# Squares of the first block's last norm on ScalarE at the second mixer's entry, and one weight split moved inside the layer norm

## The chip, the core and the metric

The kernel is one program on one core of a Trainium2 chip. Its engines run their own instruction streams in order and meet only at semaphores: TensorE (PE in the profile, PEld its weight loads) multiplies matrices into PSUM banks, VectorE (DVE) and GpSimd (POOL) do elementwise arithmetic, ScalarE (ACT) evaluates functions, and SyncE (SP) issues the loads from memory. The metric is the device time of one execution in microseconds. Times inside the kernel count from the start of the profiled span.

## What is computed

Two transformer blocks, one behind the other, on 256 tokens of width 1024. The first block (feed forward, a mixer, feed forward) ends in an RMS norm, and the second block begins with one of its own on that output, with a scale and a shift made from `c`:

```python
def first_block(x, ...):
    ...
    h = h + 0.5 * swiglu_ffn(rmsnorm(h, ffn2_norm[layer]), ffn2_w_in[layer], ffn2_w_out[layer])
    return rmsnorm(h, final_norm)

def token_mixer(h, ...):
    z = h @ w_in
    u_glu, q_lat, kv_lat, k_r, gate_logits = jnp.split(z, IN_SPLIT, axis=-1)
    ua, ub = jnp.split(u_glu, 2, axis=-1)
    u = ua * jax.nn.sigmoid(ub)
    u = causal_depthwise_conv_2(u, conv_w, conv_b)
    u = jax.nn.silu(layer_norm(u, conv_norm_g, conv_norm_b))
    y_a = u @ w_conv_out
    ...
    y_b = o @ w_attn_out
    return (g_a * y_a + g_b * y_b) @ w_out

def second_block(x, ...):
    h = rms_norm(x, g_pre_mix[l]) * (1.0 + scale1) + shift1
    y = token_mixer(h, ...)
    x = x + gate1 * rms_norm(y, g_post_mix[l])
    ...
```

## The kernel before

Activations lie transposed: 8 tiles of 128 channels by 256 tokens. Every weight passes in slabs of 128 x 2048 values through three slots (`SLOTS = 3`). For each slab SyncE loads `raw`; ScalarE rounds it to `wh` (`cast`); VectorE makes the remainder `wl = raw - wh` (`sub`, here called the weight split); TensorE multiplies the three products high x high, high x low, low x high (`wide`, 48 products a slab). Inputs are held as such pairs too: `xh` from ScalarE, `xl` from VectorE. A load waits until the slot's last split is done, so a split is also what frees `raw` for the slab three further on.

Nothing schedules the work but the order in which each engine's code is written; every wait is a semaphore count (`wait_ge(*at(name, n))`).

**The entry of the second mixer.** The first block's residual `resid` comes out of the second feed forward in four pairs of tiles (`ffn2_resid`). Two column sums of it are needed. The g sums (`g_stat`), of squares times the final gain, give the second block's norm of the first block's normed output directly: ScalarE makes eight squares (`fg_sq`, line 997), VectorE adds three pairs, TensorE sums them with a matrix of ones into bank 6 (line 2321), ScalarE takes the root, VectorE the reciprocal (`inverse("g")`), then per tile VectorE, ScalarE and VectorE make `h`, `xh`, `xl` (lines 1630, 1003, 1636), and the first gated slab takes the tiles as they come (`by_tile`). Eleven filler products (`keep_busy(11, 4)`, lines 2045 to 2050) stand between the sums and that slab. The f sums (`f_stat`), of the plain squares, are needed much later for the first block's own output: GpSimd makes four pairs of squares (`squares`, lines 658 and 736) behind the rotation angles, TensorE sums them into bank 1 behind the second gated slab (line 2041), and ScalarE copies them to `std` (`f_kept`, line 1027) in the gated unit's second step.

**The gated unit and the long convolution.** Eight slabs give four gated pairs of tiles (`glu`): ScalarE's sigmoid, VectorE's product. The 31 taps are shared out: VectorE does tiles 2 to 5 (lines 1647 to 1656), GpSimd tiles 0, 1, 6 and 7 (lines 738 to 762) behind `glu` 1, with 18 of its taps scaled by ScalarE (`scale_taps`, line 1015), which may be at most three ahead of GpSimd's addition (`tap_added`). VectorE adds the last six taps of tiles 6 and 7 once GpSimd is through (line 1764, behind `long_conv`), which gives `conv_done`.

**The layer norm.** TensorE works through the four `attn_out` slabs; behind the second one it sums the convolution's columns (`ln_mean`, line 2473, behind `conv_done`), behind the third their squares (`ln_stat`, line 2479). VectorE takes the mean off (`centre`), splits three slabs (s+3, s+4 and s+5: the last `attn_out` slab and the first two of `conv_out`), makes the reciprocal of the root and scales; then ScalarE (silu and `xh`, lines 1179 and 1182) and VectorE (`xl`, line 1793) go tile by tile, and TensorE's first `conv_out` slab takes the tiles as they come.

The order in VectorE's code there is:

```python
            centre()
            sub(s + 3)
            sub(s + 4)
            sub(s + 5)
            inverse("ln", rstd[:, :], kr_raw)
```

## Time and profile before

| | us |
|---|---|
| median of 3 runs | 1033.26 |
| lowest, highest | 1033.26, 1034.24 |
| the profiled execution, its own time | 1032.48 |
| span of that execution, first to last instruction | 1030.7 |
| TensorE busy | 1015.1 (98%) |
| VectorE busy | 794.2 (77%) |
| ScalarE busy | 497.3 (48%) |
| GpSimd busy | 510.5 (50%) |

The profile's rows are of one execution, whose time is 0.78 us below the median. A timeline row gives the start and the length in us, the engine, the line, the operation and its tiles, how many instructions are merged, and in brackets how long the engine was idle before and who released it. Tiles go by the names of the memory they lie in: many buffers share `work`, and `ps` is any PSUM bank. A product of two full-precision operands (the column sums, the fillers) appears as two passes, so five sums read as x10 there and eleven fillers as x22. Lengths of TensorE's records overlap; the distance of two starts is what one costs.

### The profile page before, as it was taken

How to read it: one execution, taken by the hardware profiler on the slowest of the kernel's cores; microseconds unless marked ns; L12 is line 12 of the kernel's file. 1: busy time of each engine (PE TensorE's matmuls, PEld its weight loads, DVE VectorE, ACT ScalarE, POOL GpSimd, SP SyncE). 2: the span in 40 equal slices, each digit the busy share in tenths (PEclk: the TensorE clock that was granted, in tenths of full speed). 3: DMA queues.
4: the chain of work that ended last, by engine and by line, in shares of the span. 5: the costliest groups of instructions: out<-in, count | busy, mean ns of one | idle time of the engine just before them, and what ended most of it. 6: DMA issues, size and time to landing. Idle time of an engine off the chain costs nothing.

```text
span 1030.7 us, 19098 instructions
## 1 busy us (share of the span) xinstructions
PE 1015.1 (98%) x7801; PEld 971.7 (94%) x7801; DVE 794.2 (77%) x799; ACT 497.3 (48%) x578; POOL 510.5 (50%) x300
## 2 busy tenths in 40 slices
PE   9999999999999999999999999999999999999997
PEld 7999999998999899999999999998999978899886
DVE  5777777699886678878677859998898787667764
ACT  6443433477532463443343656667576454343432
POOL 4576757510043027557577999999930004314400
PEclk9999999999999999999999999999999999999999
DMA  9968677646340256677677365672236517675641
GB/s 273 320 207 269 216 255 234 213 138 182 93 154 1 93 194 212 219 258 230 230 243 243 92 195 149 155 227 94 83 116 197 178 60 229 229 235 184 218 149 41
DMA packets 165997, 188.33 MB, mean 183 GB/s; under 512 B 10574, under 2 KB 155548, under 8 KB 165820
## 3 DMA queue, kind: packets, MB, share of 16 engines
q1 hardware_dynamic: 165580, 186.13, 56.8%
q0 software_dynamic: 192, 1.36, 0.4%
q8 instruction: 35, 0.57, 0.2%
q10 hardware_dynamic: 176, 0.14, 0.1%
q14 instruction: 14, 0.11, 0.0%
HBM read 186.58 MB, written 1.05 MB: 182 GB/s over the span
## 4 chain that ended last, share of the span: by engine, by line
PE 93%; DVE 4%; ACT 1%; issue 1%; DMA 0%; ACTq 0%; DVEq 0%
PE ps L1966 56%; PE ps L2010 11%; PE ps L2018 9%; PE ps L2243 2%; PE ps L1977 2%; PE ps L2189 2%; PE ps L2365 1%; PE ps L2114 1%; DVE wl L1270 1%; PE ps L2409 1%; PE ps L2058 1%; PE ps L2407 1%; PE ps L2379 1%; PE ps L2396 1%; PE ps L2048 0%
## 5 line engine op out<-in xcount | busy, mean ns | idle before, releaser
L1966 PE MATMUL ps<-xh,wh 128*128 128x256 f32 x1208 | 345.3, 286 | 3.4 <-DVE xl L1793 1.9
L1966 PE MATMUL ps<-xl,wh 128*128 128x256 f32 x1208 | 341.7, 283 | 0.0
L1966 PE MATMUL ps<-xh,wl 128*128 128x256 f32 x1208 | 341.6, 283 | 0.0
L1275 DVE TENSOR_TENSOR wl<-raw,wh 128x2048 fp32r<-128x2048 f32 x78 | 251.5, 3224 | 63.3 <-ACT wh L789 63.3
L1966 PEld LDWEIGHTS ps<-xh,wh 128*128 128x128 f32 x1208 | 231.5, 192 | 7.1 <-issue 3.9
L1966 PEld LDWEIGHTS ps<-xl,wh 128*128 128x128 f32 x1208 | 231.6, 192 | 0.5
L1966 PEld LDWEIGHTS ps<-xh,wl 128*128 128x128 f32 x1208 | 231.6, 192 | 0.0
L789 ACT ACTIVATE wh<-raw 128x2048 fp32r<-128x2048 f32 x78 | 148.9, 1911 | 148.2 <-PE ps L1966 148.2
L1270 DVE TENSOR_TENSOR wl<-raw,wh 128x2048 fp32r<-128x2048 f32 (+1 forms) x74 | 181.9, 2464 | 39.1 <-ACT wh L783 38.6
L647 POOL TENSOR_TENSOR ada_raw<-ada_raw,c_act 128x2048 f32<-128x2048 f32 x24 | 87.6, 3648 | 217.3 <-DMA ada_raw<-in_w_ada 212.2
L783 ACT ACTIVATE wh<-raw 128x2048 fp32r<-128x2048 f32 (+1 forms) x74 | 138.9, 1882 | 70.3 <-PE ps L1966 56.2
L1966 PE MATMUL ps<-yh,wh 128*128 128x256 f32 x480 | 137.6, 287 | 0.0
L1966 PE MATMUL ps<-yl,wh 128*128 128x256 f32 x480 | 135.8, 283 | 0.0
L1966 PE MATMUL ps<-yh,wl 128*128 128x256 f32 x480 | 135.8, 283 | 0.0
L650 POOL TENSOR_TENSOR ada_raw<-ada_raw 128x1024 f32<-128x1024 f32 x24 | 99.5, 4145 | 1.9
L1966 PEld LDWEIGHTS ps<-yh,wh 128*128 128x128 f32 x480 | 92.1, 192 | 0.6 <-issue 0.4
L1966 PEld LDWEIGHTS ps<-yl,wh 128*128 128x128 f32 x480 | 92.1, 192 | 0.1
L1966 PEld LDWEIGHTS ps<-yh,wl 128*128 128x128 f32 x480 | 92.1, 192 | 0.0
L2010 PE MATMUL ps<-fh,wl 128*128 128x256 f32 x320 | 89.6, 280 | 0.0
L2010 PE MATMUL ps<-fh,wh 128*128 128x256 f32 x320 | 89.6, 280 | 0.0
L2010 PE MATMUL ps<-fl,wh 128*128 128x256 f32 x320 | 89.5, 280 | 0.0
L680 POOL TENSOR_TENSOR work<-work 128x256 f32<-128x256 f32 x13 | 12.6, 971 | 132.7 <-ACT work L806 69.5
(407 smaller groups left out, 1840.0 us busy)
## 6 DMA issues: line engine op xcount, KB each, us to landing
raw<-in_ffn_w_in SPq DMA_DIRECT2D x43, 1024.0 KB, 7.5
ada_raw<-in_w_ada SPq DMA_DIRECT2D x24, 1024.0 KB, 5.3
raw<-in_ffn_w_out SPq DMA_DIRECT2D x22, 1024.0 KB, 5.0
raw<-in_w_in SPq DMA_DIRECT2D x18, 1024.0 KB, 5.4
raw<-in_w_mlp_in SPq DMA_DIRECT2D x16, 1024.0 KB, 5.5
raw<-in_w_mlp_out SPq DMA_DIRECT2D x16, 1024.0 KB, 4.9
raw<-in_w_mix_in SPq DMA_DIRECT2D x14, 1024.0 KB, 5.4
raw<-in_w_mix_out SPq DMA_DIRECT2D x4, 1024.0 KB, 5.3
```

The source lines that it names most:

```text
L647: pool.tensor_tensor(ada_raw[:, :, :], ada_raw[:, :, :], c_act[:, :].unsqueeze(2).to_broadcast([P, KT, 256]), ALU.mult).then_inc(S("ada_pa ...
L650: pool.tensor_tensor(flat[:, 0:1024], flat[:, 0:1024], flat[:, 1024:2048], ALU.add).then_inc(S("ada_part"), 1)
L783: act.activation(wh[:, s % SLOTS, 0:n], raw[:, s % SLOTS, 0:n], ACT.Copy).then_inc(high_done, 1)
L789: act.activation(wh[:, s % SLOTS, :], raw[:, s % SLOTS, :], ACT.Copy).then_inc(high_done, 1)
L1270: dve.tensor_tensor(wl[:, s % SLOTS, 0:n], raw[:, s % SLOTS, 0:n], wh[:, s % SLOTS, 0:n].bitcast(F32), ALU.subtract).then_inc(low_done, 1)
L1275: dve.tensor_tensor(wl[:, s % SLOTS, :], raw[:, s % SLOTS, :], wh[:, s % SLOTS, :].bitcast(F32), ALU.subtract).then_inc(low_done, 1)
L1966: mm = pe.matmul(bank[:, m * T:(m + 1) * T], w[:, k, m * P:(m + 1) * P], r[:, k, :], start=(m == 0 and k == 0 and j == 0), stop=(k == KT - ...
L1977: mm = pe.matmul(bank[:, m * T:(m + 1) * T], w[:, k, m * P:(m + 1) * P], r[:, k, :], start=(m == 0 and k == 0 and j == 0), stop=(k == KT - ...
L2010: mm = pe.matmul(ps[m // 2][:, (m % 2) * T:(m % 2 + 1) * T], w[:, k, m * P:(m + 1) * P], r[:, k, :], start=False, stop=False, skip_group_c ...
L2018: mm = pe.matmul(ps[n][:, :], r[:, k, tk * P:(tk + 1) * P], w[:, k, half * 512:(half + 1) * 512], start=False, stop=stop, skip_group_check ...
L2189: mm = pe.matmul(unit(bank, u % 4), lhs(u), rhs(u), start=(u % 4 == 0), stop=True, skip_group_check=True)
L2243: mm = pe.matmul(bank[:, u % 4 * CH // 2:(u % 4 + 1) * CH // 2].rearrange("p (a s) -> p a s", s=2 << i), unit(lhs, u), half_columns(unit(r ...
```

## The change

The four GpSimd squares are taken out. ScalarE makes the same four pairs of plain squares, each behind the two gained squares of its pair. TensorE sums them into bank 7, two products behind each of the first three g sums and two behind the last one; the eight sums behind the second gated slab go, and the fillers are two in place of eleven. ScalarE's copy of the sums stands behind the tiles of `xh` at the entry, and TensorE's second slab of the gated unit's second step waits for it before it writes bank 7. In the layer norm, the split of slab s+5 moves from ahead of the reciprocal to behind the second tile's low part.

```diff
--- before.py
+++ after.py
@@ -733,7 +733,6 @@
                     ins.then_inc(S("angles"), 1)
                 else:
                     step(ins)
-            squares("f", "ffn2_resid", f_squares)
             pool.wait_ge(*at("ada_taken", ADA_EARLY))
             for g, group in enumerate(POOL_TILES):
                 pool.wait_ge(*at("glu", group[-1] // 2 + 1))
@@ -995,12 +994,17 @@
             for t in range(KT):
                 act.wait_ge(*at("ffn2_resid", t // 2 + 1))
                 act.activation(qn[:, t, :], resid[:, t, :], ACT.Square, scale=final_coef[:, t:t + 1]).then_inc(S("fg_sq"), 1)
+                if t % 2:
+                    act.activation(f_squares[:, t - 1:t + 1, :], resid[:, t - 1:t + 1, :], ACT.Square).then_inc(S("f_sq"), 1)
 
             act.wait_ge(*at("g_stat", 1))
             act.activation(std[:, :], ps[6][:, 0:T], ACT.Sqrt, scale=1.0 / D, bias=eps_sq).then_inc(S("g_std"), 1)
             for t in range(KT):
                 act.wait_ge(*at("h_f", t + 1))
                 act.activation(xh[:, t, :], scaled_input(t), ACT.Identity, bias=ada[:, t:t + 1]).then_inc(S("h_xh"), 1)
+            act.wait_ge(*at("g_rstd", 1))
+            act.wait_ge(*at("f_stat", 1))
+            act.activation(std[:, :], ps[7][:, 0:T], ACT.Copy).then_inc(S("f_kept"), 1)
             cast(FIRST["glu"] + 2)
             taps_ahead = list(range(len(ACT_TAPS)))
 
@@ -1020,11 +1024,6 @@
                 scale_taps((0, 1, 1, 1)[n])
                 cast(s + 3)
                 scale_taps((0, 1, 1, 1)[n])
-                if n == 1:
-
-                    act.wait_ge(*at("g_rstd", 1))
-                    act.wait_ge(*at("f_stat", 1))
-                    act.activation(std[:, :], ps[1][:, 0:T], ACT.Copy).then_inc(S("f_kept"), 1)
                 act.wait_ge(taken, s + 2)
                 if n:
                     act.wait_ge(*at("glu", n))
@@ -1781,7 +1780,6 @@
             centre()
             sub(s + 3)
             sub(s + 4)
-            sub(s + 5)
             inverse("ln", rstd[:, :], kr_raw)
             dve.wait_ge(*at("ln_cen", 4))
             for b in range(4):
@@ -1791,6 +1789,8 @@
             for t in range(KT):
                 dve.wait_ge(*at("c_xh", t + 1))
                 dve.tensor_tensor(xl[:, t, :], conv[:, t, :], xh[:, t, :].bitcast(F32), ALU.subtract).then_inc(S("c_xl"), 1)
+                if t == 1:
+                    sub(s + 5)
                 if t == 5:
                     mix_b(3)
             sub(s + 6)
@@ -2316,19 +2316,30 @@
             ffn("ffn2", "n3", yh, yl, ("mix_resid", 4))
 
 
+            def first_block_sums(b):
+
+                pe.wait_ge(*at("f_sq", b + 1))
+                for k in (2 * b, 2 * b + 1):
+                    mm = pe.matmul(ps[7][:, 0:T], ones, f_squares[:, k, :], start=(k == 0), stop=(k == KT - 1), skip_group_check=True)
+                if b == 3:
+                    mm.then_inc(S("f_stat"), 1)
+
             for k in (0, 2, 4, 6, 7):
                 pe.wait_ge(*(at("g_add", k // 2 + 1) if k < 6 else at("fg_sq", k + 1)))
                 mm = pe.matmul(ps[6][:, 0:T], ones, qn[:, k, :], start=(k == 0), stop=(k == KT - 1), skip_group_check=True)
+                if k < 6:
+                    first_block_sums(k // 2)
             mm.then_inc(S("g_stat"), 1)
-            keep_busy(11, 4)
+            first_block_sums(3)
+            keep_busy(2, 4)
             for n in range(4):
                 s = FIRST["glu"] + 2 * n
                 if n >= 2:
                     pe.wait_ge(*at("glu", n - 1))
                 wide(s, ps[4 + 2 * (n % 2)], xh, xl, "h_xl" if n == 0 else None, one, by_tile=(n == 0))
+                if n == 1:
+                    pe.wait_ge(*at("f_kept", 1))
                 wide(s + 1, ps[5 + 2 * (n % 2)], xh, xl)
-                if n == 0:
-                    column_sums("f", lambda k: f_squares[:, k, :], KT, ps[1][:, 0:T], ("f_sq", 1), by_pair=True)
             s = FIRST["lat"]
             pe.wait_ge(*at("glu", 3))
             for n in range(3):
```

In these rows `work` is the memory of the squares and of the convolution, `con` the table with the matrix of ones, `att_col` the gains. TensorE's stream at the entry, before: the g sums and the fillers, and, where rows are left out, the first two gated slabs and then the f sums.

```order
L2114 MATMUL ps<-xh,wl 128x256
L2321 MATMUL ps<-work,con 128x256 x5
L2048 MATMUL ps<-con 128x256 x11
L1966 MATMUL ps<-xh,wh 128x256
...
L1966 MATMUL ps<-xh,wl 128x256
L2041 MATMUL ps<-work,con 128x256 x8
L1966 MATMUL ps<-xh,wh 128x256
```

The same place after, where an x counts products:

```order
L2114 MATMUL ps<-xh,wl 128x256
L2329 MATMUL ps<-work,con 128x256
L2323 MATMUL ps<-work,con 128x256 x2
L2329 MATMUL ps<-work,con 128x256
L2323 MATMUL ps<-work,con 128x256 x2
L2329 MATMUL ps<-work,con 128x256
L2323 MATMUL ps<-work,con 128x256 x2
L2329 MATMUL ps<-work,con 128x256 x2
L2323 MATMUL ps<-work,con 128x256 x2
L2048 MATMUL ps<-con 128x256 x2
L1966 MATMUL ps<-xh,wh 128x256
```

Six f sums now stand ahead of the last g sums, two behind them, and nine fillers and the later eight sums are gone. ScalarE's stream at the entry, before:

```order
L846 ACTIVATE att_col<-att_col,con 128x8
L997 ACTIVATE work<-resid,att_col 128x256 x8
L1000 ACTIVATE std<-ps,con 128x256
L1003 ACTIVATE xh<-ps,ada 128x256 x8
L783 ACTIVATE wh<-raw 128x2048 x2
...
L1015 ACTIVATE ada_raw<-work,vec 128x256 x2
L1027 ACTIVATE std<-ps 128x256
L1031 ACTIVATE hid<-ps 128x512
```

and after:

```order
L845 ACTIVATE att_col<-att_col,con 128x8
L996 ACTIVATE work<-resid,att_col 128x256 x2
L998 ACTIVATE work<-resid 128x512
L996 ACTIVATE work<-resid,att_col 128x256 x2
L998 ACTIVATE work<-resid 128x512
L996 ACTIVATE work<-resid,att_col 128x256 x2
L998 ACTIVATE work<-resid 128x512
L996 ACTIVATE work<-resid,att_col 128x256 x2
L998 ACTIVATE work<-resid 128x512
L1001 ACTIVATE std<-ps,con 128x256
L1004 ACTIVATE xh<-ps,ada 128x256 x8
L1007 ACTIVATE std<-ps 128x256
```

Four squares of 512 stand among the eight of 256, and the copy to `std` comes right behind the tiles of `xh`. VectorE's stream in the layer norm, before:

```order
L1738 TENSOR_TENSOR work<-work,rstd 128x512 x4
L1270 TENSOR_TENSOR wl<-raw,wh 128x2048 x3
L1292 RECIPROCAL rstd<-work 128x256
L1788 TENSOR_TENSOR work<-work,rstd 128x512 x4
L1775 TENSOR_TENSOR work<-ps,con 128x512
L1793 TENSOR_TENSOR xl<-work,xh 128x256 x6
L1775 TENSOR_TENSOR work<-ps,con 128x512
L1793 TENSOR_TENSOR xl<-work,xh 128x256 x2
L1270 TENSOR_TENSOR wl<-raw,wh 128x2048
```

and after:

```order
L1737 TENSOR_TENSOR work<-work,rstd 128x512 x4
L1269 TENSOR_TENSOR wl<-raw,wh 128x2048 x2
L1291 RECIPROCAL rstd<-work 128x256
L1786 TENSOR_TENSOR work<-work,rstd 128x512 x4
L1774 TENSOR_TENSOR work<-ps,con 128x512
L1791 TENSOR_TENSOR xl<-work,xh 128x256 x2
L1269 TENSOR_TENSOR wl<-raw,wh 128x2048
L1791 TENSOR_TENSOR xl<-work,xh 128x256 x4
L1774 TENSOR_TENSOR work<-ps,con 128x512
L1791 TENSOR_TENSOR xl<-work,xh 128x256 x2
L1269 TENSOR_TENSOR wl<-raw,wh 128x2048
```

The third weight split went from ahead of the reciprocal to between the second and the third low part.

## Rows read from the trace of the kernel before

**Rows 1.** page, section 4: shares of the chain that ended last, by engine

```profile
PE 93%; DVE 4%; ACT 1%; issue 1%; DMA 0%; ACTq 0%; DVEq 0%
```

**Rows 2.** timeline of TensorE, entry: start us, us, engine, line, op, out<-in, xcount

```profile
573.55 1.02 PE L2321 MATMUL ps<-work,con 128*128 128x256 f32 x4
...
576.23 4.91 PE L2048 MATMUL ps<-con 128*128 128x256 f32 x22
580.78 0.47 PE L1966 MATMUL ps<-xh,wh 128*128 128x256 f32 x1
```

**Rows 3.** chain in order of time, entry: start us, us, what, xcount

```profile
592.64 3.45 PE ps L2041 x16
```

**Rows 4.** timeline of GpSimd, squares and long convolution

```profile
585.95 8.13 POOL L661 TENSOR_TENSOR work<-resid 128x512 f32<-128x512 f32 x4
...
596.01 2.55 POOL L750 TENSOR_TENSOR work<-work,ada_raw 128x512 f32<-128x512 f32 x1 [0.74 <-ACT ada_raw L1015]
...
602.45 0.94 POOL L754 TENSOR_SCALAR con<-work,vec 128x256 f32<-128x256 f32 x2
...
604.86 2.85 POOL L754 TENSOR_SCALAR con<-work,vec 128x256 f32<-128x256 f32 x2
...
750.18 3.33 POOL L757 TENSOR_TENSOR work<-work,con 128x512 f32<-128x512 f32 x1
```

**Rows 5.** timeline of VectorE, last taps of the long convolution

```profile
753.55 5.46 DVE L1764 SCALAR_TENSOR_TENSOR work<-work,vec 128x256 f32<-128x256 f32 x12 [1.20 <-POOL work L757]
```

**Rows 6.** chain in order of time, ahead of the mean sums

```profile
741.95 17.26 PE ps L1966 x144
```

**Rows 7.** timeline of ScalarE, entry

```profile
571.16 1.71 ACT L997 ACTIVATE work<-resid,att_col 128x256 f32<-128x256 f32 x4
...
576.42 0.47 ACT L1000 ACTIVATE std<-ps,con 128x256 f32<-128x256 f32 x1 [1.04 <-PE ps L2321]
```

**Rows 8.** timeline of VectorE, entry

```profile
577.09 1.75 DVE L1292 RECIPROCAL ps<-std 128x256 f32<-128x256 f32 x1
...
585.25 0.48 DVE L1636 SCALAR_TENSOR_TENSOR xl<-ps,ada,xh 128x256 fp32r<-128x256 f32 x1 [0.15 <-ACT xh L1003]
```

**Rows 9.** timeline of ScalarE, latents of the second mixer

```profile
646.41 0.91 ACT L1015 ACTIVATE ada_raw<-work,vec 128x256 f32<-128x256 f32 x2 [1.75 <-POOL work L750]
...
650.51 1.28 ACT L1052 ACTIVATE work<-work 128x1280 f32<-128x1280 f32 x1
```

**Rows 10.** timeline of TensorE, sums of the latents

```profile
653.52 1.46 PE L2343 MATMUL ps<-work,con 128*128 128x256 f32 x6
```

**Rows 11.** timeline of VectorE, layer norm

```profile
766.25 7.23 DVE L1270 TENSOR_TENSOR wl<-raw,wh 128x2048 fp32r<-128x2048 f32 x3
773.40 1.74 DVE L1292 RECIPROCAL rstd<-work 128x256 f32<-128x256 f32 x1
...
778.19 1.10 DVE L1793 TENSOR_TENSOR xl<-work,xh 128x256 fp32r<-128x256 f32 x3
```

**Rows 12.** timeline of ScalarE, layer norm

```profile
771.17 0.47 ACT L811 ACTIVATE work<-ps,con 128x256 f32<-128x256 f32 x1 [0.61 <-PE ps L2479]
...
775.90 0.60 ACT L1179 ACTIVATE work<-work,vec 128x256 f32<-128x256 f32 x1 [2.56 <-DVE work L1788]
...
782.51 0.59 ACT L1179 ACTIVATE work<-work,vec 128x256 f32<-128x256 f32 x1
```

**Rows 13.** timeline of TensorE, first slab of conv_out

```profile
778.75 0.36 PE L1966 MATMUL ps<-xh,wh 128*128 128x256 f32 x1 [1.87 <-DVE xl L1793]
...
784.06 0.39 PE L1966 MATMUL ps<-xh,wh 128*128 128x256 f32 x1
```

**Rows 14.** timeline of the SP queue, loads behind the layer norm

```profile
773.50 22.22 SPq L492 DMA_DIRECT2D raw<-in_w_out  x4
```

**Rows 15.** timeline of TensorE, its last product

```profile
1024.46 0.39 PE L2018 MATMUL ps<-wl,xh 128*128 128x512 f32 x1
```

**Rows 16.** stretches: us, busy of five engines, PEclk, DMA share, GB/s

```profile
1026.00:1028.00 2.00, 0.00 (x0) 0.00 (x0) 1.96 (x5) 0.20 (x1) 0.00 (x0) 0.77 0.42 159
```

## Prediction

> **What bounds the kernel now.** I read the views in this order: the chain that ended last, TensorE's waits, then the timelines of each engine around the two places that the change touches. The chain is TensorE for 93% [rows 1], and at the second mixer's entry it is TensorE without a break: the squares' column sums, eleven filler products, two gated-unit slabs, then the eight sums of the first block's squares [rows 2, 3]. So products taken off TensorE are worth their length, as long as nothing else becomes late. The second thing to see is that GpSimd has a fixed stream of its own: its share of the long convolution starts once the first gated pair exists, runs from 596.01 to 753.51 and waits for nobody [rows 4]. VectorE stands idle 1.20 us for its end, adds the last taps until 759.01 [rows 5], and TensorE finishes the three slabs ahead of the layer norm's mean sums at 759.21 [rows 6]. Two independent streams meet there within 0.2 us. Whatever moves TensorE earlier than GpSimd's stream is lost there.
>
> **Entry, TensorE.** Five sums, eleven fillers and eight later sums (24 products) become 5 + 8 + 2 = 15. A product is two passes, 3.45 / 16 = 0.216 us each [rows 3]. The eight sums behind the second slab go: -3.45 us. But six of them now stand ahead of the last product of the g sums. Before, the sums start at 573.55 and the next product starts at 576.23 [rows 2]. Now 11 products have to pass: 573.55 + 22 x 0.216 = 578.30, which is 2.07 later. ScalarE isn't what holds them: its 256-wide squares follow each other by 0.41 [rows 7], four added 512-wide ones cost some 0.6 each (a 512-wide ScalarE square or copy is bounded by two 256-wide ones, 0.86), and its last square ends near 576.9, before TensorE gets there.
>
> From there the chain is serial: ScalarE's root ended at 576.89 [rows 7], the reciprocal started at 577.09, held 0.20 by a weight split [rows 8]; that slack is used up, so the reciprocal moves by 2.07 - 0.20 = 1.9, and all of h with it. Before, the first product started at 580.78 on low parts that were ready [rows 2] and the last low part ended at 585.73 [rows 8]; TensorE spends 17.26 / 144 = 0.12 a product [rows 6], 0.72 a tile, so it reached the last tile at about 586.0. Now that part ends at 587.6 and TensorE starts its last tile 0.14 later, 587.77: the first slab, and the second with it, end **1.75 us later**. The fillers are gone as cover: four products remain behind the g sums (578.30 + 4 x 0.43 = 580.0), and TensorE is idle from there to 582.4.
>
> So TensorE goes on after the second slab at +1.75 - 3.45 = **-1.70**, but the first gated pair, which needs the second slab, is at **+1.75**.
>
> **Entry, GpSimd.** The four squares leave it (8.13 us from 585.95, [rows 4]), but its next work needs the gated pair and a tap scaled by ScalarE: it already waited 0.74 us for that tap [rows 4]. The freed time buys nothing; the stream moves by +1.75. At 157.5 us of length it ends at 755.3 and VectorE's last taps at 760.8. ScalarE's copy of the sums moves to an idle place ahead of a cast (about 0.3 us, followed by a wait for TensorE): nothing.
>
> **Between.** ScalarE may scale a tap only three ahead of GpSimd, and at 646.41 it already waited 1.75 us for it [rows 9]. It now waits until 648.2; queued behind are a cast, the last latent copies and their square, which ended at 651.79 [rows 9] and would now end near 652.75. TensorE's latent sums stood at 653.52 [rows 10] and want to start at 651.8: about 1.0 us is lost, TensorE runs at -0.7 from there. The same mechanism can't make it later than GpSimd's own +1.75.
>
> **The mean sums.** TensorE arrives at 759.1 - 0.7 = 758.4 and waits until 760.9. It starts the mean sums at +1.75 to +1.85, I take **+1.8**. The -3.45 is gone and the serial delay of the entry stays.
>
> **The weight split in the layer norm.** VectorE did three splits in 7.23 us, then the reciprocal at 773.40 [rows 11], whose root was ready at 771.64 [rows 12]. With two ahead, it starts at about 771.7: -1.7. The first low part came 4.79 us after the reciprocal started [rows 11], so 776.5; the second follows by 0.34. Then the moved split (7.23 / 3 = 2.4 us) stands before the third: third low part at about 779.6 to 780.0. TensorE (which starts at 777.0 in place of 778.75, after a 1.87 us wait [rows 13]) does two tiles, stands 1.5 us, and starts its last tile at 780.1 + 5 x 0.72 = 783.7. Before, that start was 784.06 [rows 13], paced by ScalarE's tile pairs at (782.51 - 775.90) / 7 = 0.94 [rows 12]. Gain **0.4 us**: the wait is cut in two rather than removed. Bounds: -1.7 if the moved split were hidden, 0 if it cost all. I take the row-by-row value. The first of the four loads issued from 773.50 [rows 14] is freed by the moved split and goes some 6 us later; its rounding waits for a slab that ends 96 products after 778.75, so about 6 us of slack remain.
>
> **Sum.** +1.8 - 0.4 = +1.4 us. On the profiled execution: span 1030.7 + 1.4 = 1032.1, time 1032.48 + 1.4 = 1033.9; on the median 1033.26 + 1.4 = **1034.6**. 0.2% is 2.07 us, about what a measurement can tell from no change.
>
> **Rivals.**
> (A) *The saved products carry through* (faster). If GpSimd's stream shortened by 3.4 us, -1.7 - 0.4 = -2.1 would remain: 1031.1. It could only shorten by fewer collisions with VectorE: a pair of its taps takes 0.94 alone and 2.85 beside a weight split [rows 4], so two fewer. The number of splits inside the stream is the same; little speaks for it.
> (B) *One collision more* (slower): +1.9 on the stream that sets the mean sums, 1036.5. The alignment of the two engines shifts by 1.75 + 1.70 = 3.45 us, so collisions fall anew; it decides from +0.7 us.
> The Trainium skill (SBUF — State Buffer, Who interferes with whom) says that a VectorE instruction with two SBUF inputs and a GpSimd one that reads SBUF exclude each other and that issue order decides who blocks; it has no ruling on the sum, and this trace agrees by the 2.85 beside 0.94.
> (C) *TensorE's clock falls* (slower). Two new idle stretches of some 2.4 us stand at 580 and at 758.5. In this trace the granted clock is 1.00 (2.4 GHz) through a wait of 1.87 us [rows 13], but at the end, the last product over at 1024.85 [rows 15], it averages 0.77 over 1026 to 1028 [rows 16], so it had fallen to its half (1.2 GHz) by about 1027.1, 2.2 us after work stopped. At half clock each pass takes twice 0.216. Work at half clock behind either gap is on the path: between 0 and the 3.45 us of sixteen passes, I take the middle, 1.7: 1036.3, and 1038.0 if both gaps are hit.
> The Trainium skill (TensorE: Matmul & The Clock Gate, What's actually happening) says that an idle stretch sends the clock back to 1.2 GHz and that where it falls varies from run to run. By that rule, C comes in some executions and not in others.
> (D) *The change does nothing measurable at both places* (the sums hidden, the split neutral): 1033.3.
>
> **Chances.** Forecast 0.46 (own range 1033.2 to 1035.3). A 0.08. B 0.15. C 0.27. D 0.04. Faster by over 0.2% (below 1031.2): A, 0.08. Within 0.2%: forecast and D, 0.50. Slower (above 1035.3): B and C, 0.42. The range leaves out A and the case of both gaps: 1032.0 to 1037.4.
>
> **What would show it.** In the profile after: the root of the g sums starts 2.07 us after 576.42; TensorE's first slab starts near 582.4 after an idle stretch; GpSimd's first tap addition near 597.8; TensorE waits some 2.4 us ahead of the mean sums, released by VectorE's last taps (line 1763); the reciprocal 1.7 us nearer the root, and two waits of some 0.4 and 1.5 us in the first conv_out slab. The forecast is wrong if GpSimd's stream isn't some 157.5 us long, or starts before the gated pair, if the wait at the mean sums is missing, or if the granted clock drops below 1.00 behind a gap.

## The result and the profile after

The changed kernel takes 1034.83 us (median of 20 executions, 1032.99 to 1035.71), the kernel before on the same chip 1032.88 (20 executions, 1031.67 to 1035.66): a ratio of 1.0015 with a 95% interval of 1.0009 to 1.0021. That is slower, by less than the 0.2% that was set as the bound of "same". The forecast was +1.4 us; the ratio gives +1.5 (0.0015 x 1033), the two medians 1.95. The profiled execution took 1035.28 us with a span of 1033.5.

The executions are not all alike. The granted TensorE clock, averaged over an execution, is 0.997 in 16 of the 20 (1033.86 to 1035.71 us) and 0.999 or 1.0 in four (1032.99 to 1033.37). The mean is rounded to 0.001 and includes the end of the program, behind the last product, so it is only a sign of a fall in between. In the 14 traces of all kernels the sign is right: the four with a mean of 0.997 (after, x4, x9, x10) have a stretch below full clock ahead of the last product, the ten with 0.998 or more have none. The profiled execution of after is of the sixteen, and its trace has the serial delay that was forecast and, on top of it, a fall of the clock.

TensorE's timeline at the entry of after (start us, us, engine, line, op, out<-in, xcount, in brackets the idle time before and its releaser; answers to [rows 2]):

```profile
573.76 0.59 PE L2329 MATMUL ps<-work,con 128*128 128x256 f32 x2
574.19 1.02 PE L2323 MATMUL ps<-work,con 128*128 128x256 f32 x4
...
577.64 1.03 PE L2329 MATMUL ps<-work,con 128*128 128x256 f32 x4
578.51 1.03 PE L2323 MATMUL ps<-work,con 128*128 128x256 f32 x4
579.37 1.03 PE L2048 MATMUL ps<-con 128*128 128x256 f32 x4
582.74 0.36 PE L1966 MATMUL ps<-xh,wh 128*128 128x256 f32 x1 [2.34 <-DVE xl L1635]
...
583.53 0.29 PE L1966 MATMUL ps<-xh,wh 128*128 128x256 f32 x1
583.89 0.36 PE L1966 MATMUL ps<-xh,wh 128*128 128x256 f32 x1
584.05 0.41 PE L1966 MATMUL ps<-xl,wh 128*128 128x256 f32 x1
584.26 0.42 PE L1966 MATMUL ps<-xh,wl 128*128 128x256 f32 x1
...
587.25 0.35 PE L1966 MATMUL ps<-xl,wh 128*128 128x256 f32 x1
587.43 0.29 PE L1966 MATMUL ps<-xh,wl 128*128 128x256 f32 x1
```

This execution is 0.21 us late before the change begins (573.76 for 573.55). The last g sums run from 577.64 to 578.51; behind four more products TensorE stands idle for 2.34 us. It resumes at full clock, and 1.3 us later its products start 0.21 us apart in place of 0.12, from 584.05 to 587.25. The stretches of the same place (us, busy and count of PE, PEld, DVE, ACT, POOL, then PEclk, DMA share, GB/s):

```profile
580.00:583.00 3.00, 0.66 (x4) 0.29 (x3) 2.81 (x6) 0.87 (x2) 2.58 (x6) 1.00 0.79 275
583.00:586.00 3.00, 3.00 (x20) 3.00 (x20) 3.00 (x8) 1.90 (x4) 2.75 (x4) 0.66 0.00 0
586.00:590.00 4.00, 4.00 (x30) 4.00 (x30) 2.25 (x6) 3.03 (x4) 0.40 (x1) 0.83 0.00 0
...
759.00:762.00 3.00, 1.86 (x16) 1.66 (x14) 2.89 (x8) 1.04 (x1) 0.00 (x0) 1.00 0.05 14
```

PEclk 0.66 over three us and 0.83 over four are about 3.4 us at the lower level (1.2 of 2.4 GHz). At the second new idle stretch, ahead of the mean sums at 762.47, it stays 1.00. The Trainium skill (TensorE: Matmul & The Clock Gate, What's actually happening) says that an idle stretch brings the clock back to 1.2 GHz and that the point of the transition varies from run to run. This case agrees with both: by their mean clock, sixteen executions of twenty have such a fall and four have none.

GpSimd, timeline of after (answers to [rows 4]), and below it VectorE's last taps and TensorE's mean sums (answers to [rows 5] and [rows 6]):

```profile
597.53 1.09 POOL L741 TENSOR_SCALAR work<-work,vec 128x256 f32<-128x256 f32 x2 [11.13 <-DVE work L1660]
599.36 2.55 POOL L749 TENSOR_TENSOR work<-work,ada_raw 128x512 f32<-128x512 f32 x1 [0.74 <-ACT ada_raw L1019]
...
755.62 1.30 POOL L756 TENSOR_TENSOR work<-work,con 128x512 f32<-128x512 f32 x1
```

```profile
756.95 5.46 DVE L1763 SCALAR_TENSOR_TENSOR work<-work,vec 128x256 f32<-128x256 f32 x12 [2.21 <-POOL work L756]
```

```profile
762.47 3.72 PE L2484 MATMUL ps<-work,con 128*128 128x256 f32 x16 [1.61 <-DVE work L1763]
```

The squares are gone from GpSimd and it idles 11.13 us for the first gated pair; its additions run from 599.36 to 756.92, 157.56 us long, 157.5 before. The chain that ended last, page section 4, has become:

```profile
PE 77%; POOL 15%; DVE 4%; ACT 2%; issue 1%; DMA 0%; ACTq 0%; DVEq 0%; POOLq 0%
```

The 15% are that stream (157.56 of 1033.5 us). In [rows 1] TensorE had 93% and GpSimd didn't appear, although the same stream ran beside it.

The layer norm of after, VectorE, then TensorE (answers to [rows 11] and [rows 13]):

```profile
769.66 5.03 DVE L1269 TENSOR_TENSOR wl<-raw,wh 128x2048 fp32r<-128x2048 f32 x2
775.07 1.75 DVE L1291 RECIPROCAL rstd<-work 128x256 f32<-128x256 f32 x1 [0.39 <-ACT work L810]
...
779.88 0.75 DVE L1791 TENSOR_TENSOR xl<-work,xh 128x256 fp32r<-128x256 f32 x2
780.55 2.28 DVE L1269 TENSOR_TENSOR wl<-raw,wh 128x2048 fp32r<-128x2048 f32 x1
782.75 1.42 DVE L1791 TENSOR_TENSOR xl<-work,xh 128x256 fp32r<-128x256 f32 x4
```

```profile
780.44 0.36 PE L1966 MATMUL ps<-xh,wh 128*128 128x256 f32 x1 [0.17 <-DVE xl L1791]
783.22 0.39 PE L1966 MATMUL ps<-xh,wh 128*128 128x256 f32 x1 [1.11 <-DVE xl L1791]
```

One wait of 1.87 us has become two of 0.17 and 1.11. The terms of this trace add up: 0.21 us late before the change begins, 188.71 - 185.52 = 3.19 from the first g sum to the mean sums, 264.75 - 265.39 = -0.64 from there to the last product, 2.76 in all; the two profiled executions differ by 1035.28 - 1032.48 = 2.80.

### The profile page after: what moved, and what is told of

It is laid out like the page before. It is cut to its first block, busy times and chain, and to the rows that moved or that the text cites. A ratio compares the mean times of both kernels' runs of the same rounds, so it can differ in the third digit from the quotient of the medians.

```text
span 1033.5 us, 19063 instructions
## 1 busy us (share of the span) xinstructions
PE 1013.5 (98%) x7783; PEld 970.1 (94%) x7783; DVE 795.6 (77%) x799; ACT 499.6 (48%) x582; POOL 503.6 (49%) x296
## 4 chain that ended last, share of the span: by engine, by line
PE 77%; POOL 15%; DVE 4%; ACT 2%; issue 1%; DMA 0%; ACTq 0%; DVEq 0%; POOLq 0%
PE ps L1966 48%; PE ps L2010 11%; PE ps L2018 9%; POOL con L753 6%; POOL work L756 5%; POOL work L749 3%; PE ps L2243 2%; PE ps L2189 2%; PE ps L2114 1%; PE ps L2058 1%; DVE wl L1269 1%; ACT wh L782 1%; DVE work L1763 0%; PE ps L1993 0%; POOL work L741 0%
## 5 line engine op out<-in xcount | busy, mean ns | idle before, releaser
L1269 DVE TENSOR_TENSOR wl<-raw,wh 128x2048 fp32r<-128x2048 f32 (+1 forms) x74 | 178.9, 2423 | 39.2 <-ACT wh L782 38.6
L650 POOL TENSOR_TENSOR ada_raw<-ada_raw 128x1024 f32<-128x1024 f32 x24 | 96.3, 4012 | 1.9
```

Source lines behind the costliest of these rows:

```text
L650: pool.tensor_tensor(flat[:, 0:1024], flat[:, 0:1024], flat[:, 1024:2048], ALU.add).then_inc(S("ada_part"), 1)
L1269: dve.tensor_tensor(wl[:, s % SLOTS, 0:n], raw[:, s % SLOTS, 0:n], wh[:, s % SLOTS, 0:n].bitcast(F32), ALU.subtract).then_inc(low_done, 1)
```

## The experiments

Two distances of each profiled execution take out what happens elsewhere: A, from the first g sum to the start of the mean sums (serial entry, GpSimd's stream, clock there), and B, from the mean sums to the last product (the layer norm and all behind it). They also leave out how early the g sums begin, which varies from 572.40 to 573.77 us between the 14 traces though no edit touches what stands ahead of them, so two single executions can differ by over 1 us before the change begins. "Low" counts executions whose mean clock is below 0.998.

| kernel | median us | ratio, 95% | A | B | low |
|---|---|---|---|---|---|
| before | | | 185.52 | 265.39 | 32 of 105 |
| after | 1034.83 | 1.0015, 1.0009 to 1.0021 | 188.71 | 264.75 | 16 of 20 |
| x1 after, gap covered | 1033.73 | 1.0009, 1.0001 to 1.0018 | 187.63 | 264.76 | 0 of 12 |
| x2 before, gap made | 1032.36 | 0.9996, 0.9986 to 1.0006 | 185.48 | 265.38 | 2 of 12 |
| x3 split move alone | 1031.83 | 0.9992, 0.9984 to 1.0001 | 186.09* | 264.77 | 0 of 12 |
| x4 entry alone | 1035.64 | 1.0021, 1.0011 to 1.0031 | 188.73 | 265.41 | 9 of 12 |
| x8 delay, gap | 1035.66 | 1.0024, 1.0014 to 1.0034 | 187.46 | 265.38 | 6 of 9 |
| x9 delay, covered | 1035.56 | 1.0022, 1.0011 to 1.0033 | 187.40 | 266.58 | 9 of 10 |
| x11 delay, gap, split | 1034.31 | 1.0015, 1.0006 to 1.0024 | 187.41 | 264.75 | 7 of 11 |
| x5 squares behind | 1032.24 | 0.9986, 0.9975 to 0.9996 | 185.76 | 264.76 | 0 of 12 |
| x6 x5, 8 taps | 1029.90 | 0.9965, 0.9953 to 0.9977 | 184.11 | 264.77 | 0 of 8 |
| x12 x5, 7 taps | 1030.32 | 0.9974, 0.9965 to 0.9983 | 184.25 | 264.74 | 0 of 11 |
| x10 x5, 10 taps | 1033.49 | 1.0002, 0.9993 to 1.0011 | 186.00 | 266.42 | 5 of 11 |
| x7 before, 8 taps | 1033.52 | 1.0001, 0.9991 to 1.0011 | 186.25* | 265.40 | 4 of 12 |

In the two marked with *, the g sums began 1.0 to 1.2 us earlier than in before's trace, but GpSimd came to the end of its squares at the same time (593.99 in x3, 594.16 in x7, 594.08 before). The first gated pair was ready at 592.93 and 593.07, so the squares held the first tap by some 1.1 us, and the tap then met a weight split (3.2 us in place of 1.1). In x3 GpSimd's stream ends 0.58 us later after the first g sum than in before (752.94 - 572.40 against 753.51 - 573.55), which is the 0.57 in A. So the four squares on GpSimd are not free in every execution of before; in how many they hold the stream is not shown.

GpSimd's first tap in x3:

```profile
593.98 3.19 POOL L742 TENSOR_SCALAR work<-work,vec 128x256 f32<-128x256 f32 x2
```

The kernel before was run beside each set: medians 1032.83 (x1 to x4), 1033.18 (x5 to x7), 1032.82 (x8 to x10), 1033.04 (x11, x12).

### Is it the serial delay, the clock, or both

x1 puts fillers into the idle stretch of after.

```diff
             first_block_sums(3)
-            keep_busy(2, 4)
+            keep_busy(7, 4)
```

> The changed kernel with seven fillers in place of two behind the sums at the entry: 5 products of 0.43 us more, 2.16 us, which end near 582.6 where the first slab could start at 582.74. Theory (the clock falls in the idle stretch of 2.3 us and takes about 1.4 to 1.7 us from the first slab): the granted clock stays at 1.00 through the entry, the span shrinks by some 1.5 us against the executions of the changed kernel whose clock fell, and the time is 1033.0 to 1033.6, 0.3 to 0.8 us above before. Rival (the serial delay of the entry is the whole loss): the idle stretch costs nothing, the time stays at 1034.8.

The stretch shrinks to 0.19 us and no execution is low. The time, 1033.73, is 0.13 above the range that I gave and 1.1 below the rival's. A is 187.63, 1.08 us less than after's 188.71 and still 2.11 above before. TensorE and GpSimd, x1:

```profile
582.75 0.36 PE L1966 MATMUL ps<-xh,wh 128*128 128x256 f32 x1 [0.19 <-DVE xl L1635]
```

```profile
598.19 2.55 POOL L749 TENSOR_TENSOR work<-work,ada_raw 128x512 f32<-128x512 f32 x1 [0.74 <-ACT ada_raw L1019]
```

The first gated product starts where it did in after, the first addition of GpSimd 1.17 us earlier. That, or 1.08 in A, is the price of the clock on the path. With the clock held, the serial delay is what is left in A.

x2 makes a stretch of that length in the kernel before, and nothing else.

```diff
             mm.then_inc(S("g_stat"), 1)
-            keep_busy(11, 4)
+            keep_busy(4, 4)
```

> The kernel before with four fillers in place of eleven: nothing else moves, but TensorE is idle for about 2.4 us ahead of the first gated slab, from 578.1 to 580.5. Theory (the clock): in most executions the clock falls behind the stretch, for 3.4 us, and the time rises by 1.3 to 1.7 us less the 0.2 us by which the slab starts earlier: 1034.0 to 1034.5. Rival (idle stretches of this size cost nothing): 1032.7, at or 0.2 us under before.

```profile
580.34 0.36 PE L1966 MATMUL ps<-xh,wh 128*128 128x256 f32 x1 [2.42 <-DVE xl L1636]
```

```profile
580.00:583.00 3.00, 2.66 (x21) 2.69 (x22) 3.00 (x9) 1.51 (x5) 2.57 (x6) 1.00 0.56 195
```

(TensorE's timeline and a stretch of x2.) The stretch is there, 2.42 us, but the clock stayed, and only 2 of 12 executions are low. The time, 1032.36, is the rival's. My claim that a stretch of this length costs the clock in most executions was wrong here: 2.4 us earlier in the program an even longer one seldom does.

### The two parts apart

x3 is the kernel before with the split moved (the diff), x4 is after with the split put back to its old place.

```diff
             sub(s + 4)
-            sub(s + 5)
             inverse("ln", rstd[:, :], kr_raw)
...
+                if t == 1:
+                    sub(s + 5)
```

> The kernel before with the split of slab s+5 moved behind the second low part, and nothing of the entry. The prediction's step: -0.4 us, the first conv_out product some 1.7 us earlier and a new wait of 1.1 to 1.5 us ahead of the third tile. Rivals: -1.7 us if the moved split is hidden, 0 or slower if it costs all that it gives.

> The changed kernel with the split of slab s+5 back ahead of the reciprocal, so the entry alone. The prediction's step for the entry was +1.8 us on the mean sums with the clock untouched; with the clock's fall another 1.4. Both give 0.4 to 0.6 us more than the changed kernel: 1035.2 to 1035.5. Rival (the split's move is worth nothing here): the same as the changed kernel.

The split is worth 265.39 - 264.77 = 0.6 us in B, and the same from x4 (265.41) to after (264.75). In x3's own ratio it is not clear of noise (0.9984 to 1.0001). It seems to do something more: in x3, as in x1, x5, x6 and x12, which have neither the layer norm's long wait nor a long stretch at the entry, no execution is low (none of 55), while 32 of 105 of before are. No trace here is of a low execution of before, so that those lose the clock behind the layer norm's wait rests on these counts. The entry alone costs 1.0021, and the clock falls in x4's trace where it fell in after's (PEclk 0.53 from 583 to 586). So the small ratio of the whole is a loss and a smaller gain.

### Are the eight sums worth anything

x8 leaves squares and f sums where they were and only delays ScalarE's root, by six of ten fillers put among the g sums; x9 has nine fillers in place of four in the last line of the diff, and so no stretch; x11 is x8 with the split moved. (The "nine sets of four" in x9's expectation are nine fillers, x18 in its trace.)

```diff
             for k in (0, 2, 4, 6, 7):
                 pe.wait_ge(*(at("g_add", k // 2 + 1) if k < 6 else at("fg_sq", k + 1)))
+                if k in (2, 4, 6):
+                    keep_busy(2, 4)
                 mm = pe.matmul(ps[6][:, 0:T], ones, qn[:, k, :], ...)
             mm.then_inc(S("g_stat"), 1)
-            keep_busy(11, 4)
+            keep_busy(4, 4)
```

> The kernel before with its squares still on GpSimd; only ScalarE's root is put off and TensorE left with the same idle stretch as after: six of the ten fillers stand in twos ahead of three of the g sums, four behind them. The eight f sums stay on TensorE. My theory (the chain in series runs through GpSimd's stream, so all that counts is how late the first gated pair is, and the clock): about 1035.6 us, equal to the changed kernel with the split put back (1035.64), with the clock at its lower level at the first gated slab in most executions. Rival (the eight sums taken off TensorE are worth something of their own): above 1035.64, by up to the 3.45 us that they take.

> The same delay of the root in the kernel before, but with nine sets of four fillers behind it, so that TensorE doesn't stand idle ahead of the first gated slab. Theory: the serial term alone, some 1.8 us over the kernel before, so about 1034.6 to 1035.0, clock at its full level in nearly all executions. What the run before this one has on top of it is what the clock costs. Rival (the clock costs nothing): both runs of this pair come out alike within 0.3 us.

> The kernel before with ScalarE's root put off by six fillers and four fillers behind the g sums (an idle stretch of 2.3 us at the entry, as in after), and with the weight split of the layer norm moved, so that the wait of 1.9 us there is gone. The same without the split move gave 1035.66 us, at full clock in 3 of 9 executions. Theory A (the layer norm's wait of 1.9 us is where those executions lost the clock): full clock in nearly all executions and about 1033.3 us (the 1034.07 of its executions at full clock, less some 0.7 for the split). Theory B (the idle stretch at the entry is where): the lower mean clock in two thirds or more of the executions and about 1035.0 us, as after.

x8 comes out at 1035.66, x4 at 1035.64; x11 at 1034.31 with a ratio of 1.0015, after's own. A kernel with 3.45 us more work on TensorE and four squares more on GpSimd takes the same time as one without, so with the root this late the saving is worth nothing on the path. GpSimd's first addition and TensorE's mean sums in x8:

```profile
597.63 2.55 POOL L750 TENSOR_TENSOR work<-work,ada_raw 128x512 f32<-128x512 f32 x1 [0.74 <-ACT ada_raw L1015]
```

```profile
760.67 3.72 PE L2475 MATMUL ps<-work,con 128*128 128x256 f32 x16
```

The traces say it without the clock: A is 187.46 in x8 and 187.63 in x1, which has the saving. The delay alone gives 1.88 to 1.94 on A in the three traces of x8, x9 and x11, all at full clock there.

x9 missed. Its stretch is covered and its A is 187.40, as expected, but nine of ten executions are low. TensorE's timeline and two stretches of x9, in the layer norm:

```profile
779.75 0.35 PE L1966 MATMUL ps<-xh,wh 128*128 128x256 f32 x1 [1.88 <-DVE xl L1793]
```

```profile
779.00:782.00 3.00, 2.25 (x14) 2.29 (x15) 1.97 (x6) 2.90 (x7) 0.00 (x0) 0.77 0.52 166
782.00:785.00 3.00, 3.00 (x19) 3.00 (x19) 1.96 (x5) 2.91 (x7) 0.00 (x0) 0.66 0.00 0
```

The clock fell behind the wait of 1.88 us, the very wait of [rows 13] behind which it holds at 1.00 in before's trace, and B is 1.19 longer. That is a place where before's low executions can lose it too, and the split move removes it. x11 then bears on where x8's fell: with that wait gone, still 7 of 11 are low, so mostly at the entry (theory B), though its 1034.31 is 0.7 below that theory's figure. This too goes by counts: the traces of x8 and x11 are of executions at full clock. Its four others have 1032.88 to 1033.45, after's four 1032.99 to 1033.37.

### Where the saving can be had

x5 makes the f squares on ScalarE too, but behind its root, and their sums behind the g sums as part of the cover. The diff is against after, so the split stays moved.

```diff
                 act.activation(qn[:, t, :], resid[:, t, :], ACT.Square, ...).then_inc(S("fg_sq"), 1)
-                if t % 2:
-                    act.activation(f_squares[:, t - 1:t + 1, :], resid[:, t - 1:t + 1, :], ACT.Square).then_inc(S("f_sq"), 1)
...
             act.activation(std[:, :], ps[6][:, 0:T], ACT.Sqrt, ...).then_inc(S("g_std"), 1)
+            for b in range(4):
+                act.activation(f_squares[:, 2 * b:2 * b + 2, :], resid[:, 2 * b:2 * b + 2, :], ACT.Square).then_inc(S("f_sq"), 1)
...
-                if k < 6:
-                    first_block_sums(k // 2)
             mm.then_inc(S("g_stat"), 1)
-            first_block_sums(3)
-            keep_busy(2, 4)
+            keep_busy(3, 4)
+            for b in range(4):
+                first_block_sums(b)
```

> The changed kernel with the f sums behind the g sums: ScalarE makes the four plain squares behind its root (576.9 to 579.4, where it was idle 2.5 us), TensorE has three fillers and then the eight f sums, 11 products as before. So the g chain isn't delayed, no idle stretch is new, and TensorE still saves the 3.45 us behind the second slab. Theory (GpSimd's stream sets the mean sums): GpSimd's first tap addition stays within 0.3 us of 596.0, TensorE waits about 2 us ahead of the mean sums, and only the split's move is left: 1032.3 to 1032.8, 0.2 to 0.6 us under before. Rival (TensorE's saved products carry through): 3.45 us less, 1029.0 to 1029.5.

x6 is x5 with GpSimd's stream shortened by two of the taps of tiles 6 and 7, which go to VectorE; x7 is the kernel before with that alone.

```diff
-SHARED_TAPS = 6
+SHARED_TAPS = 8
```

> The same with 8 in place of 6 of the last taps of tiles 6 and 7 on VectorE: GpSimd's stream is two steps of 2.4 us shorter, VectorE's tail four instructions of 0.46 us longer, so the mean sums may start 3.0 us earlier. Theory (two streams meet at the mean sums): TensorE, 3.45 less about 1.2 us of ScalarE's wait for GpSimd ahead, is the later one again: 2.0 to 2.8 us under the variant without it, 1029.8 to 1030.6. Rival (ScalarE's hold or VectorE is the real bound): no gain over that variant.

> The kernel before with 8 in place of 6 of those taps on VectorE, nothing else. Theory (in the kernel before TensorE arrives at the mean sums within 0.2 us of the end of the last taps, TensorE being the later): a shorter GpSimd stream gains nothing, 1032.9, within 0.3 us. Rival (GpSimd's stream alone sets the end): up to 3 us less.

TensorE's mean sums in x5, in x6 and in x7:

```profile
758.69 3.72 PE L2483 MATMUL ps<-work,con 128*128 128x256 f32 x16 [1.62 <-DVE work L1763]
```

```profile
757.49 3.72 PE L2483 MATMUL ps<-work,con 128*128 128x256 f32 x16 [0.41 <-DVE work L1763]
```

```profile
758.81 3.72 PE L2473 MATMUL ps<-work,con 128*128 128x256 f32 x16 [0.41 <-DVE work L1764]
```

In x5 there is no serial delay, and what TensorE saves stands as waits, 1.28 us behind ScalarE at 645.21 and 1.62 here: A is that of before but for 0.24. In x6 the wait is 0.41 and A is 184.11, 1.4 below before; with the split's 0.6 that is 2.0 by the traces, and the time is 1029.90 us, which beats both kernels. In x7 the taps alone bring nothing: TensorE, with its eight sums still behind the slabs, gets to the mean sums 758.40 - 572.56 = 185.84 us after the first g sum, no earlier than before's 185.52. So in A neither half pays without the other. x7's median is 1033.52, 0.3 us above what I had put as its bound, with a ratio of 1.0001.

x10 and x12 look for the best share, 10 and 7 taps in the line above.

> The version with the f squares behind ScalarE's root and two more of GpSimd's taps given to VectorE came to 1029.9 us, with a wait of 0.4 us for the mean sums left. Here VectorE takes two taps more. Theory (GpSimd's stream is off the path by then and TensorE the bound): the 0.4 us that are left, so 1029.5 us. Rival (VectorE's own longer row of taps now ends last): slower than 1029.9, by up to the time of the two taps on VectorE.

> The version with the f squares behind ScalarE's root, and seven of the last taps on VectorE in place of six (1032.24 us), eight (1029.9) and ten (1033.49). In the trace with eight, GpSimd is through at 746.7, VectorE starts its own row at 750.15 behind a split and ends 0.4 us after TensorE is there. A tap on both tiles is 0.9 us on VectorE. Theory (VectorE's row ends last with eight, and GpSimd's with seven is through by 750): VectorE ends 0.9 earlier, the 0.4 us wait goes: 1029.5 us. Rival (GpSimd's stream with seven ends behind 750.2, as one more tap with its collision costs it some 3.7 us): VectorE starts when GpSimd ends, about 750.5, no gain, 1029.9 or a little more.

VectorE's own row in x10 and in x12, each with the split ahead of it:

```profile
747.90 2.29 DVE L1269 TENSOR_TENSOR wl<-raw,wh 128x2048 fp32r<-128x2048 f32 x1
750.11 9.13 DVE L1763 SCALAR_TENSOR_TENSOR work<-work,vec 128x256 f32<-128x256 f32 x20
```

```profile
748.11 3.35 DVE L1269 TENSOR_TENSOR wl<-raw,wh 128x2048 fp32r<-128x2048 f32 x1
751.38 6.37 DVE L1763 SCALAR_TENSOR_TENSOR work<-work,vec 128x256 f32<-128x256 f32 x14
```

GpSimd's last addition in x12, and a stretch of x10:

```profile
748.02 1.29 POOL L756 TENSOR_TENSOR work<-work,con 128x512 f32<-128x512 f32 x1
```

```profile
759.00:762.00 3.00, 2.71 (x9) 2.24 (x10) 3.00 (x4) 1.55 (x3) 0.00 (x0) 0.73 0.00 0
```

With ten, VectorE's row is the bound, as the rival had it: TensorE waits 2.24 us for it, and its clock falls behind that wait (PEclk 0.73 from 759 to 762); B is 1.65 longer than in x6. With seven, the row is shorter, but the split ahead of it now meets GpSimd's last addition (748.02 to 749.31) and takes 3.35 us in place of 2.29, and the row ends at 757.75, where x6's ended at 757.44. That is neither of the two ways that I had named: GpSimd is through before 750, as the theory had it, and the gain still isn't there. Both gains I had expected, 0.4 us, were missed. Eight has the lowest time of the four shares, but its 1029.90 and seven's 1030.32 come from different sets, and their intervals overlap.

## Why the prediction was right, and where it wasn't

The time was right (1034.6 for 1034.8), and so was the mechanism of the serial delay. But the prediction named its own sign of being wrong, a granted clock below 1.00 behind a gap, and that came: its likeliest case is not what most executions do. That the time still fits is in part luck.

- **Entry, serial.** Right. ScalarE's root starts 2.29 after that of [rows 7], 0.21 of it this execution's own; 2.07 was forecast:

```profile
578.71 0.47 ACT L1001 ACTIVATE std<-ps,con 128x256 f32<-128x256 f32 x1 [1.95 <-PE ps L2329]
```

  The first gated product was put at 582.4 and starts at 582.74 - 0.21. GpSimd's first addition is 1.96 us later after the first g sum in x1 and in x8 (1.75 was forecast): the reciprocal started 0.1 us behind the root's end and not at once, and TensorE, in x1, takes the tiles at the pace of the low parts, some 0.78 us each, where 0.72 had been counted. A is longer by 1.88 to 2.11 wherever only the entry was changed, with the clock held; +1.8 was forecast for the mean sums.
- **GpSimd's stream.** Right: 157.56 us long, moved by as much as the first gated pair, although it was relieved of 8.13 us of squares. (x3 and x7 show executions in which those squares do hold it. In before's trace the pair was ready at 593.99 and the squares ended at 594.08, so that there the freed time bought nothing, as the prediction had it.)
- **Between.** The mechanism was right, its place and size not. ScalarE waits for GpSimd's taps, and TensorE behind it, but a copy earlier, ahead of the sums of [rows 10]. ScalarE, then TensorE, after:

```profile
645.81 0.91 ACT L1019 ACTIVATE ada_raw<-work,vec 128x256 f32<-128x256 f32 x2 [7.00 <-POOL work L749]
646.62 1.90 ACT L782 ACTIVATE wh<-raw 128x2048 fp32r<-128x2048 f32 x1
648.43 0.57 ACT L1046 ACTIVATE work<-ps 128x512 f32<-128x512 f32 x1
```

```profile
649.05 0.39 PE L1966 MATMUL ps<-xh,wh 128*128 128x256 f32 x1 [1.23 <-ACT work L1046]
```

  In x1, where the clock doesn't blur it, TensorE gets to the latent sums level with before (forecast: -0.7), and to the mean sums 0.5 late and not 0.7 early. So it waits 1.6 us there and not 2.4. Since GpSimd sets that point, the miss changes no time. The traces tell where it comes from. At the first place the entry is late by 0.2 more than forecast, and the wait at 647.94 in x1 (1.28 us; 1.57 from start to start) costs about 0.5 more than the 1.0 forecast. At the second, the weight split of the last slab ahead of the mean sums comes second to an addition of GpSimd (750.21 to 751.50) and takes 3.38 us, from 750.27 to 753.65; TensorE stands from 753.38 to 753.80 between two products that are 0.12 apart elsewhere. In before that split came first and took 2.29, from 750.06. VectorE, GpSimd and TensorE in x1, then VectorE in before:

```profile
750.27 3.38 DVE L1269 TENSOR_TENSOR wl<-raw,wh 128x2048 fp32r<-128x2048 f32 x1
```

```profile
750.21 1.29 POOL L756 TENSOR_TENSOR work<-work,con 128x512 f32<-128x512 f32 x1
```

```profile
753.38 0.28 PE L1966 MATMUL ps<-yh,wl 128*128 128x256 f32 x1
753.80 0.35 PE L1966 MATMUL ps<-yh,wh 128*128 128x256 f32 x1
```

```profile
750.06 2.29 DVE L1270 TENSOR_TENSOR wl<-raw,wh 128x2048 fp32r<-128x2048 f32 x1
```
- **The split.** Right in kind: the reciprocal starts 1.73 us nearer the mean sums (1.7 was forecast) and right behind the root, and two waits stand for one. The second was put at 1.5 us and is 1.11, since the moved split took 2.28 and not 2.4 and the third tile was ready 0.3 earlier after the mean sums (783.22 - 762.47 = 20.75 for 21.03); the gain is 0.6 and not 0.4. The term missed what the move seems to do to the clock: it takes away a wait behind which other executions can lose it.
- **The forecast case and rival C.** The forecast's own case had the clock intact; that holds for 4 of 20 executions. In the other sixteen rival C came true, in the traces of after and x4 at the first of its two stretches, for 1.1 to 1.3 us and not 1.7 (A of after less A of x1; A of x4 less A of x8). Its chance of 0.27 stands against sixteen in twenty. It doesn't show in full in the ratio, probably because the median of before holds low executions as well, which after, with its layer-norm wait cut, no longer has in that place. With the clock held, the traces bear out the forecast's sum: x1 has 2.11 - 0.63 = 1.5 us on A and B together, for 1.4. The medians are looser: x1, all its executions, is 1.2 us above those of before in the same set that are not low (1033.73 to 1032.55), and after's own four at full clock, 1032.99 to 1033.37, only some 0.7 above. So the price of the clock is missing in the sum, and a part of it is offset by falls in before that the sum hasn't either; that the two meet near the forecast is luck.
- **Rivals A, B and D.** A (the products carry through) needs GpSimd's stream off the path; x5 and x6 show that they are worth something then and nothing without it. B (one collision more) did not come: the stream is as long as before. D fell with x4 and x8.

## What to carry to other kernels

A chain that names one engine for 93% says who was waited for last, not who is next: before taking work off it, find the stream that runs beside it without waits and see by how much it trails; here 0.2 us, and the two had to be shortened together. An idle stretch is also not always spare: two traces show the squares on GpSimd, free in before's trace, holding its stream. Work put ahead of the operand that a serial chain waits for costs nearly its full length there (2.07 us of products, 1.96 at GpSimd's first addition), so put it behind the instruction that the chain waits for, as x5 does. A stretch without work costs its own length only if the clock holds, so count in how many executions it does, and compare kernels by traces in which it does or by many executions.

## What the runs showed of the hardware that I had not expected

- The same idle stretch of TensorE brings its clock down or not by where it stands: 2.34 and 2.35 us ending between 581.98 and 582.74 in 16 of 20, 9 of 12 and 7 of 11 executions (after, x4, x11), 2.42 us ending at 580.34 in at most 2 of 12 (x2); 1.9 us in the layer norm in at most 32 of 105 executions of before, and in up to 9 of 10 of x9, where it stands 1.0 us later. These are counts of low executions; in the traces themselves the fall is seen in after, x4 and x9. By what this goes is open; no run here settles it.
- The fall can come after the engine is back at work: in after it resumed at 582.74 at full clock and slowed from 584.05 on, in x4 it resumed at 582.43 and slowed from 583.25 on.
- A weight split that meets a GpSimd addition took 3.35 us for 2.29 in x12, and so the saving of a tap was lost. The Trainium skill (SBUF — State Buffer, Who interferes with whom) has a VectorE instruction with two SBUF inputs and a GpSimd one that reads SBUF exclude each other, and the order of issue decides which one waits. The traces agree: in x12 the addition started first, at 748.02, and took 1.29, the split at 748.11 took 3.35; in before the split started first, at 750.06, and took 2.29, the addition at 750.18 took 3.33 [rows 4].
